# SSD scan of a two-layer hybrid backbone: both directions' decays in one matrix, a pass ahead for the backward states, decay preparation moved beside the gate's tiles

## The reference

```python
proj = h @ w_in
z, xbc, dt_raw = split(proj)
xbc = silu(centred_depthwise_conv(xbc, conv_w, conv_b))      # xs, B, C
dt = softplus(dt_raw + dt_bias)
# ssd_scan, for each direction (the backward one on reversed tokens):
cs = cumsum(dtc * a)                                          # within a chunk
lmat = exp(where(tri, cs[l] - cs[s], -inf))
y_diag = einsum((C B^T) * lmat, x * dt)
chunk_states = einsum(B, exp(cs[-1] - cs), x * dt)            # then carried from chunk to chunk
y_off = einsum(C, state_before_chunk, exp(cs))
# after both directions:
y = (y_f + y_b + d_skip * xs) * silu(z)
out = rmsnorm(y, g_norm) @ w_out
x = x + g2 * rmsnorm(out, norm_post)
```

## Time and profile before

| | us |
|---|---|
| median of three runs | 3347.34 |
| the profiled execution, its own time | 3349.19 |
| its span | 3347.4 |
| TensorE busy | 3031.5 (91%) |
| last conv tile through SiLU | ends at 2243.67 |
| first matmul of `soutA` | 2708.60 |
| first matmul of its third unit | 2732.28 |

### The profile page before, as it was taken

One profiled execution on the slowest core, in us unless ns is written; L12 is line 12 of the kernel. 1 busy time (PEld: TensorE's weight loads), 2 busy tenths in 40 slices (PEclk: granted clock), 3 DMA queues, 4 the chain that ended last, 5 costly groups with the idle time before them and its releaser, 6 DMA issues.

```text
span 3347.4 us, 48972 instructions
## 1 busy us (share of the span) xinstructions
PE 3031.5 (91%) x20388; PEld 2860.8 (85%) x20388; DVE 1881.6 (56%) x2666; ACT 1036.3 (31%) x1646; POOL 363.2 (11%) x231
## 2 busy tenths in 40 slices
PE   2999999987889999999999999976777789999998
PEld 2999999965789999999999989972445579999998
DVE  7567666546665556566565553773555665632334
ACT  2311134447642111442112442331111234421123
POOL 1000012000110000210000200003643312000002
PEclk9999999999999999999999999996878879999999
DMA  4445443310234444434443343220000023322223
GB/s 175 158 148 181 150 154 126 113 53 11 92 107 158 142 130 156 134 111 158 142 139 117 122 140 118 76 76 13 26 13 13 29 86 107 120 90 69 76 90 119
DMA packets 97085, 354.49 MB, mean 106 GB/s; under 512 B 10848, under 2 KB 17120, under 8 KB 96096
## 3 DMA queue, kind: packets, MB, share of 16 engines
q1 hardware_dynamic: 91232, 342.31, 30.9%
q10 hardware_dynamic: 5632, 9.05, 0.8%
HBM read 339.65 MB, written 11.67 MB: 105 GB/s over the span
## 4 chain that ended last, share of the span: by engine, by line
PE 73%; DVE 14%; ACT 6%; issue 4%; POOL 2%; DMA 1%; ACTq 0%; DVEq 0%; SPq 0%; POOLq 0%
PE P L1459 63%; DVE cv L1361 3%; DVE wl L971 2%; ACT wh L677 2%; PE P L1597 2%; DVE em L1217 1%; PE P L1386 1%; PE P L1605 1%; ACT pb L784 1%; DVE st L1095 1%; DVE xs L1233 1%; DMA mraw<-wmod_d 1%; PE P L1645 1%; PE P L1648 1%; POOL nbuf L590 1%
## 5 line engine op out<-in xcount | busy, mean ns | idle before, releaser
L1459 PE MATMUL P<-xh,wh 128*128 128x320 f32 x4016 | 1020.2, 313 | 27.5 <-DVE xl L1010 16.7
L1459 PE MATMUL P<-xl,wh 128*128 128x320 f32 x4016 | 1010.5, 311 | 0.0
L1459 PE MATMUL P<-xh,wl 128*128 128x320 f32 x4016 | 1009.9, 311 | 0.0
L971 DVE TENSOR_TENSOR wl<-raw,wh 128x1024 fp32r<-128x1024 f32 (+1 forms) x431 | 567.8, 1318 | 419.4 <-ACT wh L677 418.5
L677 ACT CAST wh<-raw 128x1024 fp32r<-128x1024 f32 (+1 forms) x431 | 482.8, 1120 | 977.3 <-PE P L1459 852.8
L1459 PEld LDWEIGHTS P<-xh,wh 128*128 128x128 f32 x4016 | 700.9, 189 | 36.1 <-DVE xl L1010 19.1
L1459 PEld LDWEIGHTS P<-xl,wh 128*128 128x128 f32 x4016 | 700.6, 190 | 0.0
L1459 PEld LDWEIGHTS P<-xh,wl 128*128 128x128 f32 x4016 | 700.4, 189 | 0.0
L590 POOL TENSOR_TENSOR nbuf<-nbuf 128x320 f32<-128x320 f32 x108 | 168.3, 1562 | 2414.8 <-ACT nbuf L692 2414.8
L1459 PE MATMUL P<-hh,wh 128*128 128x320 f32 x1408 | 381.0, 311 | 0.0
L1459 PE MATMUL P<-hl,wh 128*128 128x320 f32 x1408 | 378.4, 309 | 0.0
(11 more groups left out here) (206 smaller groups left out, 2737.0 us busy)
## 6 DMA issues: line engine op xcount, KB each, us to landing
raw<-wgu_d SPq DMA_DIRECT2D x216, 512.0 KB, 3.4
mraw<-wmod_d SPq DMA_DIRECT2D x144, 512.0 KB, 3.3
raw<-wdB_d SPq DMA_DIRECT2D x64, 704.0 KB, 4.1
raw<-wdA_d SPq DMA_DIRECT2D x32, 704.0 KB, 5.0
raw<-ain_d SPq DMA_DIRECT2D x28, 512.0 KB, 3.2
raw<-sz_d SPq DMA_DIRECT2D x26, 512.0 KB, 3.3
raw<-sx_d SPq DMA_DIRECT2D x24, 512.0 KB, 3.2
raw<-aout_d SPq DMA_DIRECT2D x16, 512.0 KB, 3.2
```

The costliest lines, as they stand in the source:

```text
L971: V.tensor_tensor(wl[:, u.u % SPLITS, 0:n], raw[:, u.u % 2, 0:n], wh[:, u.u % SPLITS, 0:n].bitcast(F32), ALU.subtract).then_inc(lo_done, 1)
L1459: ins = nc.tensor.matmul(P[:, u.banks[i], 0:C], w[:, u.u % SPLITS, k * 128:(k + 1) * 128], m[:, k, C * h:C * h + C], start=(k == 0 and w i ...
```

## The change

- **Order of units**: `sdt` comes right after the first ten gate tiles; the last six gate tiles are a phase of their own, `szB`; of `sx` the B and C tiles come first. The softplus, the sums and the decays are cut into steps `decays(m)` that stand beside the six `szB` units and the first `sx` unit on TensorE, VectorE and ScalarE.
- **Decays**: the differences cs[l] - cs[s], with the logarithm of dt, are a product of two thin matrices with 32 rows: `lk` and `rk`, split in high and low parts. They are made by 2 x 40 small products into 32-row strips (`decays`, places (5, 0) and (6, 5)); in the scan a half item is two float32r products of 32 rows and two with a mask (`segments`). Both directions' exponentials (`exps`, into `em` and `eb`) are added by GpSimd (`both`) into one matrix, so that VectorE multiplies it with C B^T once, straight from PSUM (`products`), and TensorE multiplies with x once.
- **States**: a pass ahead (`PREPASS`, 12 steps) makes all backward states and keeps them in four buffers (no spill). The contribution of both states is made in token-major form with two 512-column products, scaled by `ec` (`toff`, 128x1024 on VectorE), summed by GpSimd (`offs`), and added to y on TensorE by products with the identity.
- **Item loop**: 20 items as before, written so that each engine prepares item i+1 while it finishes item i.
- **Gate and norm**: the gate is multiplied in item by item (with 512-byte runs read back from HBM), the norm's weight is already in the spilled gate (one more ScalarE copy a tile), the squares are made item by item, and the norm's factor is folded into the post-norm that follows, with a small correction of its epsilon (`gated_floor`, and a branch in `spread` and `root`). y is split without scaling.

```diff
-CHUNKS = [(4, False), (3, False), (2, False), (0, True), (1, True), (2, True), (3, True), (4, True)]
+PREPASS = [(j, g) for j in (4, 3, 2) for g in range(GROUPS)]
+ITEMS = [(j, g) for j in range(BLK) for g in range(GROUPS)]
...
+            def decays(place, s):
+                if place == (2, 0):
+                    pe.wait_ge(sp_dve, 3)
...
+                    for j in range(BLK):
+                        ins = nc.tensor.transpose(P[:, 7, 64 * j:64 * j + 64], dtr[0:64, chunk(j)], ident[0:64, 0:64])
+                if place == (3, 0):
+                    pe.wait_ge(da_done, 1)
...
+                if place == (4, 0):
+                    pe.wait_ge(dec_exp, 2)
...
+                if place in ((5, 0), (6, 5)):
+                    t = place[0] - 5
+                    pe.wait_ge(cols_done, 1)
+                    if t == 0:
+                        pe.wait_ge(dec_exp, 3)
+                    else:
+                        pe.wait_ge(rows_done, 1)
+                    for j in range(BLK):
+                        for r in range(4):
+                            c = 128 * t + 32 * r
+                            rows = flat(3)[32 * r:32 * r + 32, chunk(j)]
+                            mm(rows, cols_d[:, j, c:c + 32], ident, start=True, stop=False)
+                            ins = mm(rows, cols_a[:, j, c:c + 32], tri[:, r % 2, :], start=False, stop=True)
...
+                    for w in range(2):
+                        r = 64 * (g % 2) + 32 * w
+                        mm(P[:, w, :], lk[r:r + 32, t, chunk(j)], rk[t][r:r + 32, 512 * hf:512 * hf + 512], start=True, stop=False)
+                    for w in range(2):
+                        ins = mm(P[:, w, :].rearrange("p (h l) -> p h l", h=4), identr, bc_mid(tmaskr[:, w, :], 4),
+                                 start=False, stop=True)
...
+            def both(i, hf):
+                pool.wait_ge(e_done, 4 * i + 2 * hf + 2)
+                m = em[:, i % 2, 512 * hf:512 * hf + 512]
+                G.tensor_tensor(m, m, eb, ALU.add).then_inc(em_add, 1)
...
+            def offs(i):
+                pool.wait_ge(offm_done, i - GROUPS + 1)
+                G.tensor_tensor(toff[:, i % 2, 0:512], toff[:, i % 2, 0:512], toff[:, i % 2, 512:1024], ALU.add).then_inc(off_sum, 1)
...
+            def take_y(i):
+                j, g = ITEMS[i]
+                dve.wait_ge(diag_done, i + 1)
+                for q in range(4):
+                    y = xs[:, 4 * g + q, chunk(j)]
+                    ins = V.scalar_tensor_tensor(y, y, dvec[:, 4 * g + q:4 * g + q + 1], P[:, 6, 128 * q:128 * q + 128], ALU.mult, ALU.add)
+                ins.then_inc(y_evac, 1)
+                dve.wait_ge(y_evac, i + 1)
+                dve.wait_ge(z_back[i % 2], 16 * (i // 2 + 1))
+                y = xs[:, 4 * g:4 * g + 4, chunk(j)]
+                V.tensor_tensor(y, y, zin[:, i % 2, :, :], ALU.mult).then_inc(y_done, 1)
```

More of the change, by code:

```diff
@@ L29 @@
 FIRST_MODS = 16
-AREA = 93696
+AREA = 95744
 NEG = -1e30
@@ L85, in units_of @@
         else:
-            units += [Unit(p, n, (0, 1), ("", n)) for n in range(p.N)]
+            order = [*range(XT, p.N), *range(XT)] if p.name == "sx" else range(p.N)
+            units += [Unit(p, n, (0, 1), ("", n)) for n in order]
         p.u1 = len(units)
@@ L197, in build @@
     jobs = attention_jobs()
-    z_units = [u for u in units if u.p.name == "sz"]
+    z_units = [u for u in units if u.p.name in ("sz", "szB")]
     ctx = ExitStack()
@@ new lines, in scan @@
+            def scan():
+                blocks(0, 0)
+                blocks(0, 1)
+                for i in range(-1, len(ITEMS)):
+                    nxt = i + 1
+                    if nxt < len(ITEMS):
+                        both(nxt, 0)
+                        if ITEMS[nxt][0]:
+                            offs(nxt)
+                        both(nxt, 1)
+                    if i >= 1:
+                        squares(i - 1)
+                    if nxt < len(ITEMS):
+                        j, g = ITEMS[nxt]
+                        if g % 2 and j + 1 < BLK:
+                            blocks(j + 1, g // 2)
+                squares(len(ITEMS) - 1)
@@ L662, in _ @@
                             add_square(PRE, s, 1, k)
-                if u.p.name == "sdt":
-                    ssd()
-                    add_gated()
+                if u.p.name == "sx" and u.u == u.p.u1 - 1:
+                    scan()
         @block.scalar
@@ L1320, in _ @@
                     V.memset(tick[:, 2:3], 0.0).then_inc(xs_done, 2)
-                if p.name != "sz":
+                if p.name not in ("sz", "szB"):
                     dve.wait_ge(unit_done, u.u + 1)
@@ L1682, in _, with gated_totals @@
+            def gated_totals():
+                pe.wait_ge(g_add, len(ITEMS))
+                for h in range(2):
+                    for b, c0 in enumerate((0, 128, 192)):
+                        ins = mm(P[:, 7, 3 * h + b:3 * h + b + 1], ssq[:, C * h + c0:C * h + c0 + 128], ones[:, 0:1], start=True, stop=True)
+                ins.then_inc(g_tot, 1)
             for h in range(2):
@@ L1690, in _ @@
                     attention(u.p)
-                if u.p.name == "sdt":
-                    ssd(u)
+                if u.p.name == "sx" and u.u == u.p.u1 - 1:
+                    scan(u)
             total(POST, last_sub, 1, KD - 1)
```

843 lines of the change are left out of this document (463 added, 380 removed).

## The result

The changed kernel took 3143.93 us (median of four runs, 3143.75 to 3147.53) beside 3348.07 us for the kernel before on the same chip: ratio 0.939, 95% interval 0.9376 to 0.9404, that is 6.1% faster. 3134 was predicted, with a range of 3085 to 3210. The profiled execution took 3143.89 us, its span is 3142.1 us: 205.3 less than before.

A forecast was written before the change was run, and what follows sets the result against it. The prediction took the scan, a chain through four engines closing once an item, to bound the kernel. Terms of -246 (scan), +37 (gate stage), -6.9 (`soutA`) and +1.7 gave -214 from 3347.34: 3134 us, range 3085 to 3210.

The forecast's parts named there:

- scan, 464.9 before: From the last convolved tile to the first `soutA` matmul: 219 us instead of 464.9, a saving of 246.
- its chunks 1 to 3 with their ends: In the scan: twelve items of 9.3 us, bound by VectorE and GpSimd, 112, plus four chunk ends, 3.
- gate stage and convolutions: Decay work beside the gate units delays the first `sx` unit and all convolutions after it: +37 us, bounds 28 to 50.
- four chunk ends, 4 x 0.7 = 3: In the scan, the transposes of B wait for the last state at each of four chunk ends: 3 us.
- no wait is near 5 us: In the item loop: the reason for expecting TensorE, busy for 83%, mostly at 2.4 GHz.
- +1.7 for the totals of squares and the post-norm: After the scan: 12 short instructions for the totals of squares and a longer post-norm cost 1.7 us.
- Idle times of 5.9, 4.1, 3.7 and 2.3: Gate stage: TensorE stalls at `szB` units 2, 4 and 5 and in the first `sx` unit, in us.
- upper bound of 50: Gate stage: the added cost in us if TensorE falls to 1.2 GHz in each stall; +37 was forecast.
- The clock did not stay down: Rival, chance 0.10: TensorE stays at 1.2 GHz in the item loop, 15 us an item, +100: 3234 us.
- 0.92 was put: In a half item of the scan: four float32r products of 512 columns, each at 0.23 us, 32-row ones included.
- the 0.5 us of the rival: Rival, chance 0.15: six array-shape changes an item cost TensorE 0.5 us each, 10.7 an item, +27: 3161 us.
- The shorter chain: Rival, chance 0.15: VectorE and GpSimd seldom meet, items are bound at 8.0 us, -24: 3110 us.

The follow-up runs named there:

- heads: The changed kernel with the edits of b_bank and cb_late together; median 3130.29 us, ratio 0.9350 to the kernel before.
- offs_pe: The changed kernel with GpSimd's `offs` taken out; TensorE adds the halves of `toff` by eight more 64-column products per item; median 3136.58 us, ratio 0.9358.
- places: The changed kernel with the five places of the decay work in TensorE's stream moved to later tenths of the same unit; median 3112.50 us, ratio 0.9292.
- alternate: The changed kernel with the four products of each half item ordered 32-row, 128-row, 32-row, 128-row instead of two and two; median 3160.94 us, ratio 0.9444.
- b_bank: The changed kernel with the transposes of B at a chunk's end moved to the PSUM bank of the x transposes; median 3143.11 us, ratio 0.9382.
- cb_late: The changed kernel with a new chunk's C B^T products moved behind the head item's second segment in TensorE's stream; median 3145.01 us, ratio 0.9389.
- heads_alternate: The changed kernel with the edits of heads and alternate together; median 3150.07 us, ratio 0.9407.
- offs_last: The changed kernel with `offs` moved behind the second `both` in GpSimd's list; median 3149.91 us, ratio 0.9406.

## Why the prediction was right, and what it missed

The mechanism was right: a loop that closed once an item has become one in which engines work side by side. The terms, against what they measured:

| term | predicted | measured |
|---|---|---|
| scan, 464.9 before | 219 | 215.9 |
| its pass ahead, fill and chunk 0 | 70 | 67.3, to the first `toff` |
| its chunks 1 to 3 with their ends | 115 | 110.8 |
| its chunk 4 and tail | 34.4 | 37.8 |
| gate stage and convolutions | +37 | +50.6 (+51.3 from the last half gate unit, which ends 0.8 earlier) |
| first two `soutA` units | -6.9 | -6.9 (2510.13 to 2526.96: 16.8) |

**The scan.** The size was right by luck, since two errors cancel. An item bound by its engines takes 8.44 us on average (heads: 101.3 / 12), not 9.3: the decay of the state took 0.68, the lower end of its bounds, and four y operations 1.12, not 1.38. But "four chunk ends, 4 x 0.7 = 3" was mis-sized: heads took away 13.3 us. That term counted TensorE's work and left out the two waits behind VectorE and the clock behind them. The reason that was given for a high clock, that no wait is near 5 us, doesn't hold: waits of 2.2 to 2.9 us were enough at two of three heads, and the first pass of the kernel before (2286 to 2328) had one of 2.9, not only the 1 to 2 that the prediction names. What bounds an item was read rightly for those with `blocks` (offs_pe), while TensorE is within 0.2 us of the bound in the others.

**Small slips.** The terms give 3133 and not 3134. The "0.9 of a float32 product at the lower clock level" is one of its two instructions; the product takes 1.8. Neither changes an argument. The +1.7 for the totals of squares and the post-norm doesn't show: from the third `soutA` unit to the end of the span both traces take 615.1 us (from 2732.28 and 2526.96).

**The gate stage.** This is the term by which the time came out 10 us above the prediction. Idle times of 5.9, 4.1, 3.7 and 2.3 were predicted, 6.47, 5.55, 5.22 and 3.82 measured: +5.1. The lower clock behind them stood only in the upper bound of 50; it cost 9.9 in this trace. The collision of `blocks` with the convolution was not foreseen at all: 3.0. On the other side, strips and small sums need 7.8 at full clock, not 11.5: I had taken 0.059 us a strip instruction from the row at the lower level, and it is 0.03 at the higher one (and 0.054 at the lower, as most of them ran here). Together +14, with 0.4 less for the strips' reading on VectorE. The statement that all of it adds to the end of the convolutions held: places took 29.6 us from the stage and all of it from the end. In three of the four idle times 1.3 us of the excess are a second table load, since ScalarE goes back to the SiLU's table for every gate unit:

```profile
2080.38 1.28 ACT L987 ACT_TABLE_LOAD   x1 [9.89 <-PE P L1577]
2081.68 0.70 ACT L987 ACTIVATE zb<-P 128x640 f32<-128x640 f32 x1
2083.63 1.28 ACT L871 ACT_TABLE_LOAD   x1 [0.39 <-ACT zb L989]
```

The sum had only the second of these. The SiLU starts 1.30 us after its load starts, so nothing beyond the load can be seen: what the Trainium skill (ScalarE: Activation LUTs, What ACT_TABLE_LOAD costs) gives as a drain on top, 1.38 us, this trace doesn't show.

**The rivals.** The clock did not stay down in the changed kernel, but 0.6 us more of TensorE in each half item was enough for 25 us of it (alternate). What the changes of shape cost in the changed kernel is small, since the four products of a half item took 1.00 us where 0.92 was put, and so the 0.5 us of the rival is too much. But the 0.92 put the two 32-row products behind each other, and they ran side by side: at 0.23 a product three of them in a row are 0.69, and some 0.15 us a change is left as an estimate. The Trainium skill (TensorEngine Tiling (Array Packing), Key Properties, and not the section that the prediction names) says that a change of tiling mode drains the engine; alternate's 1.60 us fits that, and doesn't price the change by itself. The shorter chain held in part, 8.44 against its 8.0, and was hidden by the heads.

## What to carry to other kernels

Where work for another engine is put beside a unit loop, place each piece by when its operand is ready, not at the start of a unit: here five numbers were worth 29.6 us, and a quarter to a third of it was the clock behind the waits. When a queue has two waits in a row, remove both before judging either: alone, each moved the loss (b_bank, cb_late), together they gave 13.3 us. Total times differed by a few us between runs and chips, and so did stages with waits of TensorE in them, by the clock that they met (gate stage 78.2 to 81.2, scan 213.7 to 222.1 with equal code). Stages and items without such waits repeated within 0.1 us, and small edits must be read from those.

## What the runs showed of the hardware

- After idle times of 5.55 and 6.47 us, and also after ones of 2.2 to 2.9 us at the heads of chunks 3 and 4, TensorE worked on at 1.2 GHz: the two instructions of a 512-column float32 product took 1.91 us instead of 1.02. After 2.84 and 2.62 at the head of chunk 2 it did not (clock 1.00): the length of the wait alone doesn't decide it. After idle times of 0.8 us it did not in heads; in heads_alternate it did once, with more work between. In alternate it fell behind a wait of 1.8 us and stayed low for 25 us although TensorE was busy all the time; why it didn't rise stays open.
- A GpSimd addition or product on SBUF beside a VectorE operation on SBUF slows the latter (0.68 to 1.14, 0.69 to 1.11, 3.66 to 6.69 for four); VectorE's operations with an operand in PSUM kept 0.68. The order in GpSimd's list decides which of them it meets (offs_last).
- Two 32-row products of 512 columns on different rows ran side by side: 0.50 us for both, 0.49 for one. 32-row and 128-row products in turn start 0.42 us apart; the two 128-row ones behind each other take 0.58 together (2417.34 to 2417.92). What part of this is the change itself isn't shown.
